# The MLP's up products of two token chunks by Strassen's seven block products, with a ring of half weight tiles

## The reference

```python
def channel_mixer(x, g_norm, w_up, w_down):
    h = jnp.square(jax.nn.relu(rmsnorm(x, g_norm) @ w_up))   # w_up (1024, 4096)
    return h @ w_down                                        # w_down (4096, 1024)
...
        yp = yp + mp
        ys = ys + ms
        yp = yp + channel_mixer(yp, norm_mlp[layer], w_up[layer], w_down[layer])
        ys = ys + channel_mixer(ys, norm_mlp[layer], w_up[layer], w_down[layer])
```

## Time and profile before

| | |
|---|---|
| median of three runs | 2280.75 us |
| the three runs | 2280.03, 2280.75, 2290.98 us |
| span of the profiled execution | 2288.8 us |
| its own time | not marked among the three; only 2290.98 us is above its span |
| TensorE matmuls, busy | 13982, 2258.5 us (99%) |
| VectorE busy | 1198.0 us (52%) |
| ScalarE busy | 648.3 us (28%) |
| mean granted TensorE clock | 0.989 |

### The profile page before, as it was taken

How to read it: one execution, slowest core, us unless ns; L and a number is a source line. 1 busy time by engine, 2 the same in 40 slices (tenths; PEclk the granted TensorE clock), 3 DMA queues, 4 the chain that set the end, 5 groups by cost and what they waited for, 6 DMA issues and landing times.

```text
span 2288.8 us, 32453 instructions
## 1 busy us (share of the span) xinstructions
PE 2258.5 (99%) x13982; PEld 2195.0 (96%) x13982; DVE 1198.0 (52%) x1338; ACT 648.3 (28%) x706; POOL 23.1 (1%) x39
## 2 busy tenths in 40 slices
PE   8999999999999999999999999999999999999997
PEld 8998788999999999999999998999999999999996
DVE  8777675644443444344458766544444434443445
ACT  5323632541111111111125556242111111111113
POOL 0000000000000000000000000000000000000001
PEclk9999999999999999999999999999999999999999
DMA  4334224511111111111111111111111111111102
GB/s 173 110 98 135 86 73 132 183 46 46 46 47 45 46 46 40 51 46 46 37 56 40 42 51 40 52 38 50 43 46 46 40 51 46 46 37 55 46 28 76
DMA packets 59129, 140.69 MB, mean 61 GB/s; under 512 B 6416, under 2 KB 30640, under 8 KB 59056
## 3 DMA queue, kind: packets, MB, share of 16 engines
q1 hardware_dynamic: 52720, 121.84, 16.4%
q0 software_dynamic: 3888, 14.16, 1.8%
q10 hardware_dynamic: 2448, 3.64, 0.5%
HBM read 120.62 MB, written 18.99 MB: 61 GB/s over the span
## 4 chain that ended last, share of the span: by engine, by line
PE 93%; DVE 4%; ACT 1%; issue 1%; DMA 0%; DVEq 0%; POOL 0%; ACTq 0%; POOLq 0%
PE acc L563 88%; PE ms L563 2%; DVE TT L1617 1%; PE acc L812 1%; DVE XL L1620 0%; DMA WR<-in_w_stream 0%; PE acc L890 0%; PE ms L660 0%; PE acc L827 0%; PE ms L617 0%; PE acc L823 0%; PE acc L835 0%; DVE XL L1617 0%; DVE HB L2362 0%; DVE X L1620 0%
## 5 line engine op out<-in xcount | busy, mean ns | idle before, releaser
L563 PE MATMUL acc<-XH,WH 128*128 128x352 f32 x2608 | 853.4, 327 | 9.2 <-ACT XP L1239 2.5
L563 PE MATMUL acc<-XL,WH 128*128 128x352 f32 x2608 | 840.0, 322 | 0.0
L563 PE MATMUL acc<-XH,WL 128*128 128x352 f32 x2584 | 833.9, 323 | 0.0
L1617 DVE TENSOR_TENSOR X<-X,acc 128x1056 f32<-128x1056 f32 (+1 forms) x288 | 343.2, 1193 | 370.6 <-PE acc L563 370.6
L563 PEld LDWEIGHTS acc<-XH,WH 128*128 128x128 f32 x2608 | 492.0, 189 | 21.9 <-issue 15.9
L563 PE MATMUL acc<-HH,WH 128*128 128x352 f32 x1536 | 496.6, 323 | 1.4 <-DVE X L1617 1.4
L563 PE MATMUL acc<-HH,WL 128*128 128x352 f32 x1536 | 495.9, 323 | 0.0
L563 PE MATMUL acc<-HL,WH 128*128 128x352 f32 x1536 | 495.3, 322 | 0.0
L563 PEld LDWEIGHTS acc<-XL,WH 128*128 128x128 f32 x2608 | 494.6, 190 | 0.2
L563 PEld LDWEIGHTS acc<-XH,WL 128*128 128x128 f32 x2584 | 487.3, 189 | 0.0
L1114 ACT ACTIVATE WH<-WR 128x1024 fp32r<-128x1024 f32 x177 | 182.8, 1049 | 624.0 <-PE acc L563 561.6
(11 more groups left out here) (337 smaller groups left out, 1337.1 us busy)
## 6 DMA issues: line engine op xcount, KB each, us to landing
WR<-in_w_stream SPq DMA_DIRECT2D x152, 512.0 KB, 3.3
WR<-in_w_stream POOLq DMA_DIRECT2D x27, 512.0 KB, 4.1
X<-in_x_t SPq DMA_DIRECT2D x8, 528.0 KB, 9.6
LA<-in_x_t SPq DMA_DIRECT2D x24, 176.0 KB, 2.5
xz_scratch<-LA SPq DMA_DIRECT2D x24, 176.0 KB, 1.8
X<-xz_scratch SPq DMA_DIRECT2D x8, 528.0 KB, 5.6
out_y_t<-X SPq DMA_DIRECT2D x12, 352.0 KB, 2.4
u_scratch<-UR SPq DMA_DIRECT2D x4, 576.0 KB, 3.0
```

What stands on the lines that cost most here:

```text
L563: return pe.matmul(out, lhs, rhs, start=start, stop=stop)
L1617: return dve.tensor_tensor(out, a, b, op)
```

## The change

The up part of an MLP step is computed for its two tiles of hidden rows together. For token chunks 0 and 1 the weights of the step form 2 x 2 blocks (two tiles of hidden rows, two halves of the 1024 inputs), and so does X (two halves, two chunks): their product takes seven block products of sums and differences instead of eight. Chunk 2 stays as it was.

TensorE runs 11 segments of 4 k x 3 passes = 12 matmuls (`segment`): b11, p1, t1, b21, p2, t2, b22, t3, p1, n4, p2. Four products are summed in one bank (B_CHAIN), out of which ScalarE takes a `snapshot` after the first, second and third; VectorE puts the blocks together (c11, c12, p5, c22, c21), and applies max and RS (f0 and f1 read chunk 2 of either tile). Then come the 8 down outputs of the step before, each as before.

Weights come from an array of their own, w_mlp, into the two buffers WR (F0 and F1). They are split by `units` of 512 columns into a ring of six half tiles; for the up part there are eight units of a step, four of them sums or differences that VectorE forms first (in F0 or in the former constants' tile cst). Four units hold the down weights, and each of them takes 256 columns of both F0 and F1. X is written before each MLP as 36 parts of 352 columns (high and low), most of them in the rows of XH and XL, some in free space. The hidden tiles are squared once, in place (`squared`), then rounded into two slots of HH (`rounded`), after the down product before has ended. `lam` moves from ahead of the first MLP to behind `residual(2)`.

`mark` counts TensorE's segments and down outputs (19 a step), `evict` VectorE's readings of banks (14 a step: c11, f0, c12, c22, c21, f1, eight adds), `u_ready` the units split. The core of the diff (SP's loads, TensorE, ScalarE's step, VectorE's residual, its pieces and the order of a step):

```diff
+RING, SPARE, NRING = (3, 0, 1), 2, 6
+F0, F1 = 1, 0
...
+STEP_MARKS, STEP_EVS, STEP_UNITS = UP_MARKS + DOWN_MARKS, 6 + KT, 12
+AFTER = {"u0": 2, "u1": 3, "u2": 5, "u3": 6, "u4": 7, "u5": 8, "u6": 9, "u7": 11,
+         "d0": 13, "d1": 15, "d2": 17, "d3": 19}
...
+        W_A11, W_A12 = WR[:, F0, 0:UNIT], WR[:, F0, UNIT:2 * UNIT]
+        W_A21, W_A22 = WR[:, F1, 0:UNIT], WR[:, F1, UNIT:2 * UNIT]
+        W_SUM = cst[:, :]
+        B_CHAIN, B_P24 = ms[:, 0, 0:XW], ms[:, 1, 0:XW]
+        B_P3, B_F0, B_F1 = acc[:, 1, 0, 0:XW], acc[:, 1, 1, 0:XW], acc[:, 0, 0, 0:XW]
...
+        def down_source(j):
+            return WR[:, :, 2 * P * j:2 * P * (j + 1)]
...
+                with sp.Fori(0, HG - 2) as i:
+                    load(F0, i * 4 + 4, i * STEP_UNITS + (8 + 6))
+                    load(F1, i * 4 + 5, i * STEP_UNITS + (8 + 8))
+                    load(F0, i * 4 + 6, i * STEP_UNITS + (8 + 12))
+                    load(F1, i * 4 + 7, i * STEP_UNITS + (8 + 12))
...
+                    ready(0)
+                    if not first:
+                        pe.wait_ge(evict[layer], evs - 1)
+                    segment(B_CHAIN, u0, "b11", True, False, True, wait=first)
+                    if first:
+                        read_wait(pe, "oute6" if layer == 0 else "outo6")
+                        read_wait(pe, "oute7" if layer == 0 else "outo7")
+                    segment(B_F0, u0, "p1", True, False, wait=first)
+                    ready(1)
+                    pe.wait_ge(snap, 3 * HG * layer + snaps + 1)
+                    segment(B_CHAIN, u0 + 1, "t1", False, False, True, wait=first)
+                    if first:
+                        norm_row(r)
+                    ready(2)
+                    segment(B_P24, u0 + 2, "b21", True, True, wait=first)
...
+                    segment(B_CHAIN, u0 + 5, "t3", False, True, True, wait=first)
+                    ready(6)
+                    if not first:
+                        pe.wait_ge(evict[layer], evs)
+                    segment(B_F1, u0 + 6, "p1", True, False)
+                    ready(7)
+                    pe.wait_ge(evict[layer], evs + 1)
+                    segment(B_P24, u0 + 7, "n4", True, True, wait=first)
+                    segment(B_F1, u0 + 7, "p2", False, True)
...
+                        pe.wait_ge(evict[layer], evs(m))
...
+                with pe.Fori(0, HG - 1) as i:
+                    units, evs = i * STEP_UNITS + 8, i * STEP_EVS + 6
+                    up(8, units, evs, i * 3 + 3)
+                    down(16, units + 8, lambda m: evs + (3 if m == 0 else 6 if m == 1 else 5 + m), i * 2 + 2)
...
+                def rounded(u, tiles, free):
+                    act.wait_ge(mark[layer], free)
+                    act.wait_ge(h_sq, FT * layer + tiles)
...
+                    snapshot(layer, 2, m + 6)
+                    down_hi(layer, 0, 16, m + AFTER["u2"], i * 32 + 48)
+                    down_hi(layer, 1, 17, m + AFTER["u3"], i * 32 + 48)
+                    down_hi(layer, 2, 18, m + AFTER["u4"], i * 32 + 48)
+                    squared(0, i * 2 + 3)
+                    down_hi(layer, 3, 19, m + AFTER["u5"], i * 32 + 48)
...
+                    following(0, "u6")
+                    following(1, "u7")
+                    squared(1, i * 2 + 4)
...
+                    add_to_residual(order[j], ACC[name])
+                    read_wait(dve, name)
+                    if j < 4:
+                        front(j)
+                    else:
+                        temps(j - 4)
+                    if j:
+                        sum_square(r, j)
+                    if layer == 1 and j < 4:
+                        lo_w(STREAM[f"outo{j}"] + SLOTS)
+                    if j in ((1, 3, 5) if layer == 0 else (4, 5, 6)):
+                        at = 2 * (1, 3, 5).index(j) if layer == 0 else 2 * (j - 4)
+                        up_lo(layer, at, at, at + 1, 16)
+                        up_lo(layer, at + 1, at + 1, at + 2, 16)
+                    if j == KT - 2:
+                        for i in range(4):
+                            rest(i)
+                        for i in range(3):
+                            pair(i)
...
+                def c22(m):
+                    dve.wait_ge(mark[layer], m + 8)
+                    tt(t1[:, chunk[0]], B_CHAIN, s1, ALU.subtract)
+                    relu(t1[:, chunk[1]], B_CHAIN, chunk[1]).then_inc(evict[layer], 1)
+                def c21(m, e):
+                    dve.wait_ge(mark[layer], m + 10)
+                    dve.wait_ge(evict[layer], e + 4)
+                    tt(t1[:, chunk[0]], t1[:, chunk[0]], B_P24, ALU.add).then_inc(evict[layer], 1)
+                def f1(m, e):
+                    dve.wait_ge(mark[layer], m + 11)
+                    relu(t1[:, chunk[2]], B_F1, chunk[2]).then_inc(evict[layer], 1)
+                    dve.wait_ge(evict[layer], e + 6)
+                    relu(t1[:, chunk[0]], t1[:, chunk[0]], chunk[0]).then_inc(t_ready, 1)
...
+                    c11(m, e, n)
+                    f0(m)
+                    unit_lo(layer, 16, u + 9, down_source(0))
+                    unit_lo(layer, 17, u + 10, down_source(1))
+                    c12(m, e, n)
+                    unit_lo(layer, 18, u + 11, down_source(2))
+                    p5(n)
+                    c22(m)
...
+                    following(0)
+                    c21(m, e)
+                    following(1)
+                    f1(m, e)
...
+                    add(0)
```

## The result

The changed kernel takes 2375.31 us (median of 4 runs, 2370.09 to 2381.17), the kernel before on the same chip 2285.86 us (4 runs, 2280.03 to 2291.33): ratio 1.0387, 95% interval 1.0355 to 1.042. It is slower, as forecast, but by 89 us instead of 34, and outside the range.

The account below looks back on a forecast made before the run. The prediction took TensorE's matmul pace, 0.1600 us each, to bound the MLP. Its terms, -61.4 + 60 + 17.5 + 5.8 + 6.0 + 2.5 + 3.6 = +34, on a median of 2280.75 gave 2314 us; 8-in-10 range 2274 to 2340.

Parts of the forecast that it names:

- Fewer matmuls: Up part of the MLP steps: 384 matmuls go at 0.1600 us each, -61.4 us.
- The new wait in every step: Second down product (d1): TensorE waits 2.0 us for f1 in thirty steps, +60 us, 36 to 81.
- Before the first step: Each layer's MLP start: TensorE waits behind VectorE's longer residual code, +12 us in layer 0 and +5.5 in layer 1.
- First steps: First step of each layer: c21 behind units 11 and 12, then ScalarE's squared(1) and roundings; twice 2.9, +5.8 us.
- Last steps: Last down product of each layer: nothing covers the hidden tiles' roundings; twice 3.7 less the former 1.44, +6.0 us.
- Odd layer: Odd layer: a weight split ahead of an add, and lam()'s activations ahead of take_xb(0), cost +2.5 us (0 to 5).
- Clock: TensorE's granted clock falls behind the two long gaps only, some 1.8 us lost each, +3.6 us.
- rival 3: The clock falls in each step: each of the 30 waits costs 1.8 us more, +54, 2368 us; chance 0.06.
- Rival 1: At d1 on f1: the loop's wait is hidden and the kernel is faster, -26, 2255 us; chance 0.11.

Follow-up runs that it names:

- experiment 1: The changed kernel with c21 and f1 moved ahead of the next step's units 20 and 21 on VectorE; 2268.62 us, ratio 0.9919 to the kernel before.
- Experiment 4: Four kernels, each the kernel before with only idle time of TensorE put into the MLP steps; 2327.73, 2371.06, 2378.38 and 2432.94 us.
- e4: The kernel before with two idle ScalarE writes holding up the sixth down output, TensorE idle 2.25 us per step; 2378.38 us, ratio 1.0397.
- e8: The kernel before with three idle ScalarE writes holding up the sixth down output, TensorE idle 3.24 us per step; 2432.94 us, ratio 1.0653.
- e1: The changed kernel with c21 and f1 ahead of the next step's units 20 and 21 on VectorE (experiment 1); 2268.62 us, ratio 0.9919.
- e5: The kernel before with one idle ScalarE write holding up the sixth down output, TensorE idle 1.12 us per step; 2327.73 us, ratio 1.0162.
- e9: The kernel before with one idle ScalarE write ahead of each of the third and sixth down outputs, idle 1.12 + 1.19 us per step; 2371.06 us, ratio 1.0379.

## Why the prediction was wrong

The sign, and the places and lengths of the waits, came out; the size did not.

- **Fewer matmuls**, -61.4: right. 13598 matmuls, and with nothing in their way a step of 44.2 us (experiment 1).
- **The new wait in every step**, +60: right in mechanism and place, a little small. The wait stands at d1, released by f1, in each of the 30 steps. Its row says 2.1 us on average; by the matmul starts it costs 2.4, 30 x 2.4 = 72, inside the stated 36 to 81. I had 3.3 us for the first tile where it took 3.8 in the step shown; the second was in 5.0 us after the first one's issue instead of 5.2, and did not decide; and what a gap costs beyond its row, some 0.27, was left out. The estimate of 3.2 us by the Trainium skill's fit (page "DMA: Bandwidth & Descriptors", section "Anatomy of one DMA") was further off; the page gives that fit for DMAs issued from GpSimd, and these are issued by SP.
- **Before the first step**, 17.5: 12.2 + 5.7 = 17.9. **First steps**, 5.8: 2.2 twice and 0.3 twice, 5.0. **Last steps**, 6.0: 3.7 twice less 1.4. **Odd layer**, 2.5: from the end of layer 0's last down product to the start of layer 1's MLP the kernel takes 316.0 us against 314.2, so 1.8. That is partly luck: behind the 2.46 us gap in this stretch the clock fell in the trace before and not in the one after, so the change itself cost some 3.4.
- **Clock**, +3.6: **this step failed.** The prediction put the fall "behind the two long gaps" and no others. It came behind 22 of the 30 step waits, and also behind the layer starts and both last down products: 22 x 1.7 = 37 in the loops and some 6 outside. That is rival 3, "the clock falls in each step", to which I gave 0.06 and 2368 us; 2375 was measured. It was not quite each step, and a fall costs 1.5 to 1.7 instead of 1.8.

Why I put it so low: the rows showed a fall after 2.46 us idle and none after 1.44, and my wait of 2.0 lay between, nearer to the 2.46. The argument that set the chance was that TensorE works 44 us without a break between waits. Experiment 4 shows that this is no protection: over 44 us of work without a break lie between the gaps of `e4` and `e8` too. With two points and a value between them the honest chance was near one half. And the fall after 2.46 us was a single case, of a gap behind which the clock fell in six traces of eleven. The "TensorE: Matmul & The Clock Gate" page of the Trainium skill, in the table of the section named in the prediction, sets its warning at idle gaps longer than these waits; the runs differ from it, since 36 of 58 gaps of 1.65 to 2.3 us (21 of 28 in the changed kernel's loops, 15 of 30 in `e4`) had a fall behind them. The measurement decides.

The sum again with what was measured: -61.4 + 72 + 37 in the loops, 23 at the layer starts, 6 at the last down products, 6 of clock outside the loops, 2 in the odd layer: +85, against 90.5 between the two spans. Of the rest, 2.8 us lie ahead of the first MLP (474.15 against 471.3; in `e1` it is 471.3 again, so that is not of the change), and some 2 are what the eight gaps outside the loops cost beyond their rows. About 1 us is not placed.

Rival 1 (the wait hidden, 2255) was the right price for a kernel with another order on VectorE: `e1` is that kernel and takes 2269. Of the 14 us between, 4 are the kernel before, which was 2284.4 us in that batch, and some 4 the clock and what gaps cost beyond their rows, outside the loops; some 6 are not placed.

## What to carry to other kernels

Before pricing a wait, ask why the instruction that ends it stands where it does in its engine's queue: here two reads of PSUM stood behind work that needed a DMA, and moving them was worth more than the algorithm's whole saving. Look at the next place down the queue as well, since an order that mends one product can starve the one behind it. And price each idle stretch of TensorE twice, for itself with the 0.27 us that its row leaves out, and for the clock behind it: where a trace has a fall at one length and none at a shorter one, a wait between them carries a good part of that price.

## What the runs showed of the hardware

- Behind idle stretches of 1.65 to 2.3 us the granted clock falls in some cases and not in others: 21 of 28 in the changed kernel, 15 of 30 in `e4`, there nearly in every other step. Behind 3.24 us it was 29 of 30, behind 1.12 to 1.21 us (`e5`, `e9`) 0 of 90. In these loops the shortest idle stretch with a fall was 1.83 us, the longest without one 3.24; at the same length either can be. What decides between them is open.
- A fall is short: ten or so matmuls 0.29 us apart, then full pace, 1.5 to 1.7 us in all.
- The idle time that a row gives is less than the gap costs: 1.12 costs 1.39, and 2.22 costs 2.5.
- The times of one kernel's executions go with this clock. Of 32 executions of the kernel before, the shortest span, 2275.3 us, had a mean granted clock of 0.996 to 0.998, the longest, 2294.4 us, one of 0.987.
